# Other addresses and orders of reading for TensorE's weights and activations in a two-block transformer kernel

## The reference, cut to what matters

```
proj = h @ w_in[l]                      # 1024 x 2594
mixed = concat(nsa_mixer, gla_mixer, pool_mixer)
h = layer_norm(ALPHA * h + mixed @ w_out[l])
ff = square(relu(h @ w_up[l])) @ w_down[l]     # 1024 x 4096 x 1024
h = layer_norm(ALPHA * h + ff)
```

```
h = h + 0.5 * rms_norm(swiglu(rms_norm(h), wi, wo))    # 1024 x 5632, 2816 x 1024
h = h + rms_norm(mixer(rms_norm(h)))                   # layer 0 dilated, layer 1 windowed attention
h = h + 0.5 * rms_norm(swiglu(rms_norm(h), wi2, wo2))
h = h + rms_norm((p @ ple_proj) * sigmoid(rms_norm(h) @ ple_gate))
```

## Time and profile before

| | |
|---|---|
| median of 2 runs | 3377.64 us (3377.63 to 3377.66) |
| span of the profiled execution, first to last instruction | 3375.9 us |
| TensorE busy | 3332.4 us, 99% |
| weight loads (beside the matmuls) | 2654.5 us |
| VectorE, ScalarE, GpSimd busy | 1821.0, 1241.4, 331.0 us |
| granted TensorE clock, mean | 1.000 |
| read from HBM | 296.14 MB, 88 GB/s over the span |

### The profile page before, as it was taken

The page is one execution under the profiler, slowest core; times in us unless marked ns, Lnnn a source line. Parts: engine busy times, 40 slices in busy tenths (PEclk is TensorE's granted clock), DMA queues, the critical chain, the costliest instruction groups (busy, mean ns, idle before and its releaser), DMA issues.

```text
span 3375.9 us, 43189 instructions
## 1 busy us (share of the span) xinstructions
PE 3332.4 (99%) x16894; PEld 2654.5 (79%) x16894; DVE 1821.0 (54%) x2938; ACT 1241.4 (37%) x1882; POOL 331.0 (10%) x242
## 2 busy tenths in 40 slices
PE   9999999999999999999999999999999999999999
PEld 7767888776788887888777778888888876788887
DVE  6676334557742446443666664435644357654436
ACT  3354222424541324332333342324432235532325
POOL 0310000222100020000223100000000012000001
PEclk9999999999999999999999999999999999999999
DMA  4112222311122232223322122232222321122232
GB/s 165 62 43 72 99 95 100 124 63 51 51 95 99 95 105 75 100 93 106 114 69 69 63 83 98 95 104 100 88 94 99 106 96 45 57 100 99 98 107 82
DMA packets 81433, 300.39 MB, mean 89 GB/s; under 512 B 9040, under 2 KB 9040, under 8 KB 80640
## 3 DMA queue, kind: packets, MB, share of 16 engines
q1 hardware_dynamic: 78624, 284.20, 24.9%
q0 software_dynamic: 1568, 11.98, 0.9%
q10 hardware_dynamic: 1088, 2.10, 0.2%
HBM read 296.14 MB, written 2.10 MB: 88 GB/s over the span
## 4 chain that ended last, share of the span: by engine, by line
PE 90%; DVE 4%; ACT 2%; issue 1%; POOL 1%; DMA 0%; POOLq 0%; ACTq 0%; DVEq 0%
PE bank L917 26%; PE bank L919 25%; PE bank L918 25%; PE bank L961 2%; PE bank L968 2%; PE bank L962 2%; PE bank L1243 1%; PE bank L1224 1%; DVE wl L2147 1%; PE bank L1483 1%; PE bank L1495 1%; ACT wh L1646 1%; PE bank L1538 1%; ACT sc L1818 1%; PE bank L1258 1%
## 5 line engine op out<-in xcount | busy, mean ns | idle before, releaser
L917 PE MATMUL bank<-x,wh 128*128 128x512 f32 x2616 | 1046.2, 400 | 3.3 <-DVE wl L2147 2.0
L919 PE MATMUL bank<-x,wl 128*128 128x512 f32 x2616 | 1020.0, 390 | 0.0
L918 PE MATMUL bank<-x,wh 128*128 128x512 f32 x2616 | 1019.0, 390 | 0.0
L1646 ACT ACTIVATE wh<-raw 128x1024 fp32r<-128x1024 f32 x526 | 555.8, 1057 | 1127.5 <-PE bank L919 1076.3
L2147 DVE TENSOR_TENSOR wl<-raw,wh 128x1024 fp32r<-128x1024 f32 x526 | 673.1, 1281 | 534.1 <-ACT wh L1646 532.9
L917 PEld LDWEIGHTS bank<-x,wh 128*128 128x128 f32 x2616 | 491.2, 188 | 123.7 <-issue 22.7
L919 PEld LDWEIGHTS bank<-x,wl 128*128 128x128 f32 x2616 | 491.0, 188 | 103.9
L918 PEld LDWEIGHTS bank<-x,wh 128*128 128x128 f32 x2616 | 491.7, 188 | 97.9 <-issue 3.8
L917 PE MATMUL bank<-mid,wh 128*128 128x512 f32 x1216 | 474.9, 391 | 0.5 <-DVE wl L2147 0.5
L918 PE MATMUL bank<-mid,wh 128*128 128x512 f32 x1216 | 473.1, 389 | 0.0
L919 PE MATMUL bank<-mid,wl 128*128 128x512 f32 x1216 | 473.1, 389 | 0.0
(11 more groups left out here) (375 smaller groups left out, 3351.3 us busy)
## 6 DMA issues: line engine op xcount, KB each, us to landing
raw<-stream SPq DMA_DIRECT2D x526, 512.0 KB, 3.3
raw_apart<-stream SPq DMA_DIRECT2D x12, 512.0 KB, 3.7
sm<-small POOLq DMA_DIRECT2D x2, 2144.0 KB, 10.8
tb<-tab POOLq DMA_DIRECT2D x2, 1728.0 KB, 15.0
h<-x_t ACTq DMA_DIRECT2D x4, 512.0 KB, 6.9
out_t<-h SPq DMA_DIRECT2D x8, 256.0 KB, 2.7
tba<-tab_a POOLq DMA_DIRECT2D x1, 1152.0 KB, 7.6
pf<-p_t POOLq DMA_DIRECT2D x2, 512.0 KB, 4.9
```

The source lines that it names most:

```text
L917: pe.matmul(dst, hi, src[:, kc, 0, :], start=start, stop=False)
L918: pe.matmul(dst, hi, src[:, kc, 1, :], start=False, stop=False)
L919: return pe.matmul(dst, lo, src[:, kc, 0, :], start=False, stop=stop)
L1646: act.activation(high_of(n)[:, :], raw_of(n)[:, :], ACT.Copy).then_inc(hi_done, 1)
```

## The change

Nothing is added, dropped or moved in any engine's order: there are as many instructions on each engine as before, in the same order. What changes is where operands lie and in which order TensorE walks over them, in three ways.

1. **Weights.** The host writes blocks 6 and 7 of each unit interleaved: column 0 of block 6, column 0 of block 7, column 1 of block 6, and so on (`in_pair`). TensorE reads the stationary operand of chunk 6 or 7 at every second element, 8 bytes apart, over 1024 bytes (`columns`). This holds for all units, so for `x`, `mid`, `ao` and `bo` alike, and in `abreast` too. Blocks 0 to 5 are as before.
2. **Order of lines.** In `piece`, where the source is `x`, chunks 4 and 5 are read in another order of 16-byte lines (four elements): chunk 4 all even lines and then all odd ones, chunk 5 lines 0, 4, 8, ..., then 1, 5, 9, ... and so on. The bank is written in the same order, so each result lands where it did (`lines`, `LINES`). `abreast`, `mid`, `ao` and `bo` don't have this.
3. **`mid`.** Each row of 512 columns of `mid` takes 521 places, so a rounded part and its remainder lie 2084 bytes apart in place of 2048 and a chunk 4168 bytes after the one before. The starts of three rows in four are no longer at a multiple of 16 bytes.

```diff
--- before.py
+++ after.py
@@ -86,6 +86,7 @@
 
 BY_POOL, BY_PE, BY_DVE = (0, 1), (2, 3, 4, 5), (6, 7)
 END_BANKS = (5, 6, 7, 3)
+LINES = {4: 2, 5: 4}
 HALF = (slice(0, S // 2), slice(S // 2, S))
 
 
@@ -450,7 +451,7 @@
         vec = at("vec", [P, V_N])
         place[0] += (x_at - place[0]) % 512
         mix_at = place[0]
-        mid = at("mid", [P, FF2C, 2, S], F32R)
+        mid = at("mid", [P, FF2C, 2, S + 9], F32R)[:, :, :, 0:S]
         assert place[0] <= 229368, place[0]
 
 
@@ -911,12 +912,26 @@
         def _(pe):
             c = Count(pe)
 
+            def columns(t, k):
+
+
+                if k < 6:
+                    return t[:, k * P:k * P + P]
+                return t[:, 6 * P:8 * P].rearrange("p (c two) -> p two c", two=2)[:, k - 6, :]
+
+            def lines(ap, src, kc):
+
+
+                n = LINES.get(kc, 1) if src is x else 1
+                return ap if n == 1 else ap.rearrange("p (a o w) -> p o a w", o=n, w=4)
+
             def piece(dst, u, col, src, kc, start, stop):
 
-                hi, lo = high_of(u)[:, col:col + P], low_of(u)[:, col:col + P]
-                pe.matmul(dst, hi, src[:, kc, 0, :], start=start, stop=False)
-                pe.matmul(dst, hi, src[:, kc, 1, :], start=False, stop=False)
-                return pe.matmul(dst, lo, src[:, kc, 0, :], start=False, stop=stop)
+                hi, lo = columns(high_of(u), col // P), columns(low_of(u), col // P)
+                dst, xh, xl = (lines(t, src, kc) for t in (dst, src[:, kc, 0, :], src[:, kc, 1, :]))
+                pe.matmul(dst, hi, xh, start=start, stop=False)
+                pe.matmul(dst, hi, xl, start=False, stop=False)
+                return pe.matmul(dst, lo, xh, start=False, stop=stop)
 
             def free_tile():
 
@@ -955,8 +970,7 @@
 
                 if t == 0:
                     c.wait(x_hi)
-                at_ = slice(kc * P, kc * P + P)
-                hi, lo = high_of(u + t)[:, at_], low_of(u + t)[:, at_]
+                hi, lo = columns(high_of(u + t), kc), columns(low_of(u + t), kc)
                 dst = bank[c.homes[t][0]][:, :]
                 pe.matmul(dst, hi, x[:, kc, 0, :], start=kc == 0, stop=False)
                 pe.matmul(dst, lo, x[:, kc, 0, :], start=False, stop=False)
@@ -964,7 +978,7 @@
                     return
                 c.wait(x_ready)
                 for i in range(width):
-                    dst, hi = bank[c.homes[i][0]][:, :], high_of(u + i)[:, at_]
+                    dst, hi = bank[c.homes[i][0]][:, :], columns(high_of(u + i), kc)
                     mm = pe.matmul(dst, hi, x[:, kc, 1, :], start=False, stop=kc == 7)
                     if kc == 7:
                         mm.then_inc(unit_done, 1)
@@ -2984,6 +2998,14 @@
             for w in (t[:, :, :part], t[:, :, part:])]
 
 
+def in_pair(stream):
+
+
+    t = stream.reshape(-1, P, 4, 2, P).copy()
+    t[:, :, 3] = t[:, :, 3].transpose(0, 1, 3, 2).reshape(-1, P, 2, P)
+    return t.reshape(-1, P, UNIT)
+
+
 def weight_stream(a):
     units = []
     z = np.zeros
@@ -3038,7 +3060,7 @@
         units += ffn(1)
         units.append(tiles(a["ple_proj_2"][l]).reshape(2, 4, P, 256).transpose(0, 2, 1, 3).reshape(2, P, UNIT))
         units.append(tiles(a["ple_gate_2"][l]))
-    return np.concatenate(units, 0)
+    return in_pair(np.concatenate(units, 0))
 
 
 def small_weights(a):
```

## The result

The changed kernel takes 3417.12 us (median of 2 runs, 3417.08 to 3417.16), the kernel before 3377.64 us. The ratio is 1.0117, with a 95% interval of 1.0101 to 1.0133: 39.5 us more. That is inside 2% and inside the wide range given (3295 to 3466 us), but outside the forecast's own range of 3370 to 3400 us, and eight times the 4.8 us that the sum allowed for the three edits together.

The account below looks back on a forecast made before the run. TensorE, busy 99% of the span, was taken to bound the kernel through its dense matmul steps. 3375.9 + 0 + 0 + 4.8 = 3380.7 us, plus 1.7 for runs, 3382.4, said as 3383 us; own range 3370 to 3400, wide 3295 to 3466.

Parts of the forecast that it names:

- the sum: Whole kernel: span of 3375.9 us plus 0, 0 and 4.8 us for the three edits, 3380.7 us.
- The count of 12480: Dense matmuls in `piece` and `abreast`: 12480 at 226.67 ns make 2829 us, 84% of the span.
- A: Loads of chunks 6 and 7: each line of weights holds the stream by one column; +40 us, 3417 us; 10%.
- the 13.3 ns: Dense matmul steps: excess over 213.3 ns for 512 columns, 167 us in all, put down to SBUF's rate of lines.
- Interleaved weights, 0: 2976 loads of chunks 6 and 7: longer reading stays covered by a matmul, value 0; 7 us at worst.
- Order of lines, 0: Chunks 4 and 5 over `x`, 1962 matmuls: still 128 lines each, so 0; 185 us from above.
- VectorE's 94.5: Upper price for reordered matmuls over `x`: 128 lines at VectorE's 0.74 ns, 94.5 ns a matmul, 185 us in all.
- `mid` 36 bytes on, 4.8 us: Over `mid`: one more line, 1.77 ns, on 2736 of 3648 matmuls, 4.8 us.
- The float32 matmul of the earlier trace: Plain float32 matmul of 512 columns: two span 1.02 us, so a step of 0.43 us without the excess.
- B: Chunks 4 and 5 over `x`: line order breaks the stream, 94.5 ns a matmul, +185 us, 3563 us; 20%.
- C: Over `mid`: rows off the line are fetched twice, up to 620 us, 3998 us; 5%.
- D: Dense matmuls: the excess is a clash of two streams at fixed relative addresses; other offsets save, 3303 or 3274 us; 15%.

Follow-up runs that it names:

- the first kernel: Not the model: 53 groups of 24 float32r matmuls of 512 columns with a weight load each, one thing varied per group; unvaried 226.7 ns a step.

## Why the prediction was right or wrong

**Right.** What bounds the kernel: only the step of a dense matmul could move the time, and only that moved. The count of 12480 and the step of 226.67 ns, which chunks 0 to 3 kept but for their first. The distance of 1.7 us between span and runs (1.8 now). That a load would last 188 to 212 ns and never hold a matmul back for its weights. And that the result would be within 2%, though not for the reason given: each part alone costs some four times what the sum had for all three together, and 22 us of it overlap. That the total stayed below 67.6 us, and that it fell on A's 3417, is luck as far as the prediction goes.

**The step that failed** is the inference from the 13.3 ns: "the moving stream is held by how fast SBUF gives lines, whichever they are". It rested on one agreement, 1.77 ns per line here and 1.8 ns on VectorE, from two engines. One group of another size, which this kernel doesn't have, would have refuted it: the excess is 13.3 ns at 256, 384 and 512 columns alike and 19.9 at 448, where a rate gives 6.7, 10.0, 13.3 and 11.7. All three prices hung on it. What the runs show in its place is a step that depends on how the moving operand lies relative to the weights: 233.3 ns with it 32 bytes on, 226.9 with both.

- *Interleaved weights, 0.* The load was covered and its length forecast well. But "covered" was read as "free". It cost 20.3 us alone, in the mean some 6.7 ns for each such load. In the end these are half of A's 13.3 ns, and not by A's reason.
- *Order of lines, 0.* 19.1 us alone. Over the 1962 reordered matmuls that is 9.7 ns each, neither 0 nor VectorE's 94.5, and the affected matmuls weren't 1962 but also those behind them.
- *`mid` 36 bytes on, 4.8 us.* 21.8 us alone. The count of lines was beside the point: a pad of 32 bytes, which adds none, costs 16.8.
- *The float32 matmul of the earlier trace rows.* The two rows of 1.02 us are one matmul and not two: in the first kernel 24 such matmuls leave 48 rows, 429.1 ns apart. No term hung on it.
- *The sum.* Three terms of 20, less 22 us of overlap.

**The rivals.** A is refuted where its number was met. B's sign was right and its place too narrow; its reason, from the Trainium skill (Advanced Engine Details and Errata, "PSUM Cachelines"), that any non-contiguous pattern slows matmuls, is not what happened: the bank alone in an order by twos or fours, or by twos in pairs of elements, takes 226.7 ns, as in sequence. The page's other sentence, that pairs suffice, agrees with that. B's other reason, that an order of reading can hit the same place each time, isn't refuted: by sixteens is longer even with no load beside. C isn't what cost here: over `mid`, with the pad alone, the rows that start at a line took 231.9 ns in the mean and the others 232.1 to 234.6, so none in four was spared. D had the mechanism, two streams that clash at fixed relative addresses, and the wrong sign: it took the base's 13.3 ns for the clash and any other offset for the cure. Read in sequence over 512 columns, offset 0 is the best of all that were tried; only together with the order by fours is another one better.

The chance given to D was too low for its reason: the earlier trace rows, one modelled end with no load beside, was taken as an argument against any effect of loads. A second reason was the Trainium skill (SBUF — State Buffer, "Who interferes with whom"), cited under A, by which TensorE's two reads have independent ports. The ports may be independent, which no run here can show; that the two reads leave each other's time alone, as the prediction took from it, isn't so for `float32r`: 233.3 ns with the moving operand 32 bytes on, 226.9 with the weights on as well.

## What to carry to other kernels

Work that is hidden beside other work isn't free until the covering work has been seen at the same length with and without it; compare the steps from start to start, not busy time or durations. Where two reads run side by side on the same engine, treat their relative address as a size to be measured: here 64 bytes and an order of lines, with no instruction more, are worth just under 2%, and a pad chosen without looking costs 0.6%. An excess over the ideal should be measured at a second size before it is called a rate, and at a third before it is called a constant.

## What the runs showed that was not expected

- In many of the steady groups the step is 220.0, 226.7 or 233.3 ns, though others lie between (223.3, 229.1, 231.1): 213.3 and one, two or three times 6.67 ns, which are 16 columns at 2.4 GHz. Why is open.
- Reading every second element of the moving operand doubles the step, to 453 ns (L144 above). The Trainium skill (Advanced Engine Details and Errata, "SBUF Cachelines") says that at least two hits on a 16-byte line are needed to absorb the latency; for the `float32r` stream two don't suffice, it wants all four.
- The same kernel can settle at either of two steps: order by fours has 223.3 and 226.7 ns in one trace, and its four runs lie near 3358.0 and near 3362.6 us, where seven runs of the kernel before agree to 0.8.
